# Attention in a two-block transformer kernel: one VectorE pass writes the masked, scaled scores to four SBUF places

## The reference

```
scores = q . k * 96 ** -0.5        # for one head: 1024 queries x 1024 keys
scores = where(key <= query, scores, -inf)
p      = exp(scores - max over keys) ; p = p / sum over keys
out    = p @ v
```

## Time and profile before

| | us |
|---|---|
| median of 3 runs | 2840.65 (2839.79 to 2842.64) |
| profiled execution, its own time | 2838.5 |
| span of its instructions | 2836.8 |
| PE busy | 2729.4 (96%) |
| DVE busy | 1814.4 (64%) |
| ACT busy | 1021.3 (36%) |
| POOL busy | 1277.9 (45%) |

### The profile page before, as it was taken

One profiled execution on the slowest core, in us unless ns is written; L12 is line 12 of the kernel. 1 busy time (PEld: TensorE's weight loads), 2 busy tenths in 40 slices (PEclk: granted clock), 3 DMA queues, 4 the chain that ended last, 5 costly groups with the idle time before them and its releaser, 6 DMA issues.

```text
span 2836.8 us, 32978 instructions
## 1 busy us (share of the span) xinstructions
PE 2729.4 (96%) x12578; PEld 2155.0 (76%) x12578; DVE 1814.4 (64%) x2070; ACT 1021.3 (36%) x1397; POOL 1277.9 (45%) x780
## 2 busy tenths in 40 slices
PE   7999999999999999999998999889998999999998
PEld 5888788787777888887786887555587788878777
DVE  3111355655747766669879758776637766777887
ACT  4000323332214333334444014665535433344444
POOL 2433322223436988884333444102332888833321
PEclk9999999999999999999999999999899999999999
DMA  5223232324442333336631534103333345565543
GB/s 180 96 95 108 88 119 90 119 90 156 148 141 79 100 112 102 90 118 215 205 115 49 187 112 117 33 33 97 102 127 104 119 141 163 173 206 163 163 134 134
DMA packets 336967, 348.90 MB, mean 123 GB/s; under 512 B 18915, under 2 KB 256602, under 8 KB 336822
## 3 DMA queue, kind: packets, MB, share of 16 engines
q1 hardware_dynamic: 327254, 311.30, 35.6%
q10 hardware_dynamic: 9568, 35.66, 3.2%
HBM read 237.53 MB, written 108.34 MB: 122 GB/s over the span
## 4 chain that ended last, share of the span: by engine, by line
PE 51%; DVE 10%; issue 2%; ACT 2%; DMA 1%; POOL 1%; SPq 0%; DVEq 0%; ACTq 0%; POOLq 0%
PE ps L3282 34%; PE ps L533 9%; DVE op_lo L3359 2%; PE ps L2367 1%; PE ps L2740 1%; DVE sw_lo L3192 1%; PE ps L2390 1%; DVE small L2321 1%; PE ps L2377 1%; DVE x L2312 1%; PE ps L2858 1%; DVE acc L3603 1%; DVE acc L3610 0%; PE ps L2713 0%; DVE acc L1889 0%
## 5 line engine op out<-in xcount | busy, mean ns | idle before, releaser
L3282 PE MATMUL ps<-op_hi,sw_hi 128*128 128x512 f32 x1769 | 692.6, 392 | 15.5 <-DVE op_lo L3359 8.2
L3282 PE MATMUL ps<-op_hi,sw_lo 128*128 128x512 f32 x1769 | 689.1, 390 | 0.0
L3282 PE MATMUL ps<-op_lo,sw_hi 128*128 128x512 f32 x1769 | 688.9, 389 | 0.0
L499 POOL TENSOR_TENSOR w_hi_t<-w_raw,ones 128x1024 fp32r<-128x1024 f32 (+1 forms) x85 | 162.1, 1910 | 735.7 <-PE ps L533 354.7
L3282 PEld LDWEIGHTS ps<-op_hi,sw_hi 128*128 128x128 f32 x1769 | 332.4, 188 | 96.8 <-issue 16.8
L3282 PEld LDWEIGHTS ps<-op_hi,sw_lo 128*128 128x128 f32 x1769 | 332.4, 188 | 69.2
L3282 PEld LDWEIGHTS ps<-op_lo,sw_hi 128*128 128x128 f32 x1769 | 332.6, 188 | 68.7 <-issue 0.5
L656 DVE TENSOR_TENSOR stage<-ps,rstd 128x1024 f32<-128x1024 f32 x62 | 75.8, 1222 | 345.4 <-PE ps L533 326.9
L3182 ACT ACTIVATE sw_hi<-sw_sumNone 128x512 fp32r<-128x512 f32 (+1 forms) x252 | 157.1, 624 | 330.3 <-PE ps L3282 247.0
L533 PE MATMUL ps<-h1hi,w_hi_t 128*128 128x512 f32 x720 | 233.5, 405 | 13.0 <-DVE h1lo L617 9.0
L3192 POOL TENSOR_TENSOR sw_lo<-sw_sumNone,sw_hi 128x512 fp32r<-128x512 f32 x138 | 214.7, 1565 | 33.2 <-ACT sw_hi L3182 33.1
(11 more groups left out here) (444 smaller groups left out, 4877.2 us busy)
## 6 DMA issues: line engine op xcount, KB each, us to landing
op_raw<-hidden SPq DMA_DIRECT2D x42, 1024.0 KB, 8.6
w_raw<-in_w_in SPq DMA_DIRECT2D x60, 512.0 KB, 3.9
sw_raw<-in_w_ffn_in SPq DMA_DIRECT2D x44, 512.0 KB, 5.3
proj<-stage ACTq DMA_DIRECT2D x42, 512.0 KB, 2.6
hidden<-hidden_blocks SPq DMA_DIRECT2D x13, 1536.0 KB, 6.2
acc<-proj SPq DMA_DIRECT2D x36, 512.0 KB, 4.5
hidden<-hidden_blocks SPq DMA_DIRECT2D x14, 1280.0 KB, 5.0
sw_raw<-in_w_up SPq DMA_DIRECT2D x32, 512.0 KB, 8.3
```

Source lines behind the costliest of these rows:

```text
L499: ins = pool.tensor_tensor(whi[:, u.par, s], raw[:, u.par, s], ones[:, 0:1].to_broadcast([P, n]), ALU.mult)
L3282: mm = pe.matmul(out, w, x[:, k, :], start=(k == 0 and i == 0 and r < 4), stop=(k == n - 1 and i == 2), skip_group_check=r >= 4)
```

## The change

DVE takes the scores with one instruction, `tensor_tensor_reduce`: out = (scores + mask_row) * (-scale), with the minimum over the row as a second output (starting from BIG). `out` is one of four places `x4[:, n % 4]` in SBUF. Since everything is negated, the minimum is minus the scaled maximum, and it serves as the bias as it stands. ACT takes the exponential of (bias minus that place), in place. The mask is now a row of 1024, zero but for the last 128 columns; its last N columns are added to the whole of the scores. POOL makes it in the earlier stage, behind L1944. `scores(n + 2)` waits for the pass of `n` (`s_stat`) and no longer for the exponential; the pass of `n` waits for `turn(n - 4)` (`pt_ready`). The small columns move (`sm`), `turned_p` gets places of its own, and two waits of the mLSTM on `p_ready` are on `s_stat`.

```diff
+        mask_row = at("mask_row", [P, T], R0 + 128)
...
                     pool.memset(cb[:, :, 0:3], 0.0).then_inc(S["ml_consts"], 1)
+                    pool.memset(mask_row[:, :], 0.0).then_inc(S["ml_consts"], 1)
+                    pool.wait_ge(S["ml_consts"], 2)
+                    last = mask_row[:, T - P:T]
+                    pool.affine_select(out=last, in_=last, compare_op=ALU.is_ge, fill=-BIG, base=0,
+                                       pattern=[[-1, P]], channel_multiplier=1).then_inc(S["ml_consts"], 1)
...
-        turned_p = [x4[:, 2, :], x4[:, 3, :]] + [at(f"p_turned{n}", [P, T], kb)[:, :] for n, kb in ((2, 107.5), (3, 111.5))]
+        turned_p = [at(f"p_turned{n}", [P, T], kb)[:, :] for n, kb in enumerate((75.03125, 107.5, 79.03125, 111.5))]
...
-                act.wait_ge(S["s_stat"], 2 * n + 2)
-                if n >= 2:
-                    act.wait_ge(S["pt_ready"], n - 1)
-                act.activation(x4[:, n % 2, 0:N], PS[n % 2][:, 0:N], ACT.Exp, bias=sm(n, 1), scale=QK_SCALE,
-                               accum_out=sm(n, 2)).then_inc(S["p_ready"], 1)
+                act.wait_ge(S["s_stat"], n + 1)
+                act.activation(x4[:, n % 4, 0:N], x4[:, n % 4, 0:N], ACT.Exp, bias=sm(n, 0), scale=-1.0,
+                               accum_out=sm(n, 1)).then_inc(S["p_ready"], 1)
...
+            dve.wait_ge(S["ml_consts"], 3)
+            dve.wait_ge(S["q_rope"], 8)
             for n, (h, i) in enumerate(NQ):
                 N = (i + 1) * P
                 dve.wait_ge(S["s_ready"], n + 1)
-                late = PS[n % 2][:, N - P:N]
-                dve.tensor_tensor(late, late, negm[:, :], ALU.add).then_inc(S["s_masked"], 1)
-                dve.wait_ge(*count("s_masked", n + 1))
-                dve.tensor_reduce(sm(n, 0), PS[n % 2][:, 0:N], AX.X, ALU.max).then_inc(S["s_stat"], 1)
-                dve.wait_ge(S["s_stat"], 2 * n + 1)
-                dve.tensor_scalar(sm(n, 1), sm(n, 0), -QK_SCALE, None, ALU.mult).then_inc(S["s_stat"], 1)
+                if n == 3:
+                    dve.wait_ge(S["vh_t"], 8)
+                if n >= 4:
+                    dve.wait_ge(S["pt_ready"], n - 3)
+                dve.tensor_tensor_reduce(x4[:, n % 4, 0:N], PS[n % 2][:, 0:N], mask_row[:, T - N:T], -QK_SCALE, BIG,
+                                         ALU.add, ALU.min, sm(n, 0)).then_inc(S["s_stat"], 1)
...
-                    pe.wait_ge(S["p_ready"], n - 1)
+                    pe.wait_ge(S["s_stat"], n - 1)
```

More of the change, by code:

```diff
@@ L246 @@
          "out_row": ("kdt_ready", 8), "x3_squared": ("g_step", 24), "x3_summed": ("conv_step", 16), "qk_high": ("yb_ready", 8),
-         "qk_low": ("yb_scaled", 8), "s_masked": ("o_sum", 8),
+         "qk_low": ("yb_scaled", 8),
          "x3_last_spilled": ("mv_loaded", 64)}
@@ L2227, in mla_act @@
                 if h == 7:
-                    act.activation(small[:, 44:45], ones[:, 0:1], ACT.Exp)
+                    act.activation(small[:, 52:53], ones[:, 0:1], ACT.Exp)
                 act.wait_ge(S["unit_done"], uk.times(1, 1))
@@ L2257, in sm @@
         def sm(n, what):
-            c = 40 + 5 * (n % 2) + what
+            c = 40 + 3 * (n % 4) + what
             return small[:, c:c + 1]
@@ L2309, in normalise @@
                 dve.wait_ge(S["p_ready"], n + 1)
-                dve.reciprocal(sm(n, 3), sm(n, 2)).then_inc(S["rs_inv"], 1)
+                dve.reciprocal(sm(n, 2), sm(n, 1)).then_inc(S["rs_inv"], 1)
                 dve.wait_ge(S["rs_inv"], n + 1)
-                dve.tensor_scalar(x4[:, n % 2, 0:N], x4[:, n % 2, 0:N], sm(n, 3), None, ALU.mult)\
+                dve.tensor_scalar(x4[:, n % 4, 0:N], x4[:, n % 4, 0:N], sm(n, 2), None, ALU.mult)\
                    .then_inc(S["p_norm"], 1)
+            dve.wait_ge(S["ml_consts"], 3)
+            dve.wait_ge(S["q_rope"], 8)
             for n, (h, i) in enumerate(NQ):
@@ L2376, in turn @@
                 for j in range(NQ[n][1] + 1):
-                    tr = pe.transpose(PS[2][:, j * P:(j + 1) * P], x4[:, n % 2, j * P:(j + 1) * P], ident[:, :])
+                    tr = pe.transpose(PS[2][:, j * P:(j + 1) * P], x4[:, n % 4, j * P:(j + 1) * P], ident[:, :])
                 tr.then_inc(S["pt_ready"], 1)
@@ L2679, in turn_v @@
             if h == 0:
-                pe.wait_ge(S["p_ready"], 64)
+                pe.wait_ge(S["s_stat"], 64)
             if h == 1:
@@ L2691, in weight_scores @@
             if n == 0:
-                pe.wait_ge(S["p_ready"], 63)
+                pe.wait_ge(S["s_stat"], 63)
             if J == 0:
```

## The result

| us | before | after |
|---|---|---|
| median of 6 runs each | 2840.86 (2839.79 to 2843.09) | 2826.53 (2819.55 to 2829.75) |
| profiled execution, its own time | 2838.5 | 2826.9 |
| span | 2836.8 | 2825.2 |

The ratio after to before is 0.9946, 95% interval 0.9933 to 0.9959. It is worked out from all runs; the two medians are 14.3 us apart (0.9950), where 9.5 was forecast. So the sign and the place were right, and the size was forecast too small.

A forecast was written before the change was run, and what follows sets the result against it. PE, busy for 96% of the span, was taken as the bound, so only its idle time could be won: 9.4 + 0.4 - 0.3 = 9.5 us less, 2829.0 us profiled, 2831.2 as median, forecast range 2827 to 2835.

The forecast's parts named there:

- the place: The one stage touched, 1780 to 1953.5 us, where PE lost 19.4 us to other engines inside the steps.
- the sum over PE's waits: In the steps, fourteen waits give 0.40 us each and twelve 3.79 together: 9.4 us less (7.6 to 10.1).
- the scores' gate: The scores' two waits for the exponential, 1.0 us, go as PSUM frees earlier; together 0.4 us won.
- the ring: In the steps PE and DVE wait for each other: transposes 15.5 us for DVE, DVE 35.1 for scores.
- The pass's rate: The new DVE pass costs what the running maximum costs: 1225 ns for 1024, 291 for 128.
- The first rival: The new DVE pass runs at half rate, as the scan does: slower, 2845.6 us, median 2847.8; chance 0.13.
- term s: What DVE's chain to the reciprocal loses per step: 0.44 - 0.05, about 0.40 us, ends 0.30 and 0.45.
- From N = 896 on PE's own work covers DVE's: In the steps' widest score rows, from N = 896 on, PE was said not to wait for DVE.
- the 26 waits: PE's transposes waiting for DVE's row multiplication, 15.5 us in all; fourteen above 0.45 us, twelve below 0.40.
- POOL's mask row: Filling the mask row on POOL in the earlier stage, 1.0 to 1.9 us; loss 0 to 1.2, taken 0.3.
- The whole shift should be passed on: The mLSTM behind the steps starts from their end, so the full 9.5 us should reach the total.
- the second rival: Gain made, but PE's clock takes part: one more low stretch of 10 us, 2836.2 us; chance 0.10.

The follow-up runs named there:

- e7: Changed kernel with two small DVE operations more (128 and 64 columns) between pass and reciprocal; 2846.09 us, ratio 1.0017 to the kernel before.
- e9: Changed kernel with one small DVE operation more (128 columns) between pass and reciprocal; 2830.22 us, ratio 0.9969 to the kernel before.
- e1: The changed kernel measured again without any edit; 2828.40 us, ratio 0.9957 to the kernel before, steps 159.6 us.
- e4: Kernel before without the mask's addition on DVE, so its output lacks the causal mask; 2831.68 us, ratio 0.9973 to the kernel before.
- e5: Changed kernel with the scores waiting for the exponential again, as before; 2825.56 us, ratio 0.9952 to the kernel before.
- e3: Changed kernel with three extra PE matmuls, results unused, at the start of the steps; 2828.02 us, ratio 0.9955 to the kernel before.
- e10: Changed kernel with four mLSTM pieces on DVE moved from steps 52, 53, 56 and 57 to 58 to 61; 2821.65 us, ratio 0.9933 to before.
- e12: The changed kernel measured once more without any edit; 2825.36 us, ratio 0.9947 to the kernel before, steps 157.1 us.
- e6: Changed kernel with two SBUF places in place of four, the pass waiting for the transposes of n - 2; 2845.01 us, ratio 1.0017 to before.
- e11: Kernel before with its exponential writing to four places in place of two, nothing else; 2839.80 us, ratio 1.0003 to the kernel before.
- e8: Kernel before with two extra PE matmuls, results unused, filling the idle gap at the steps' start in time; 2840.38 us, ratio 0.9998.

## Why the prediction was right in kind and wrong in size

The step that failed is the sum over PE's waits: 9.4 us, 9.8 with the scores' gate, where the steps got 13.9 us shorter at an equal clock. Both of its inputs were too small: what the chain loses, and what each wait is worth.

**The place and the ring.** Right. PE lost time in the steps only where its work ended before DVE's chain; a shorter chain shortened these waits (15.5 to 6.3 us) and turned up as DVE's wait for the scores (35.1 to 44.2). A longer chain brought them back (e7, e9).

**The pass's rate.** Right: 1225 ns for 1024, the maximum's. The Trainium skill, "DVE: opcode table, instruction layouts, handler registers and perf-mode slots", Datapath and trigger behaviour, says that a stage reading its own last result loses no cycle; the trace agrees, the slope is (1225 - 292) / 896 = 1.04 ns an element. The halving that the Trainium skill names in "Vector Engine (DVE) Microarchitecture Reference", Points that are easy to get wrong, is for two sources in SBUF; with one in PSUM the trace shows none. The first rival, half rate, is out.

**The term s was mis-sized.** The prediction put 0.05 us for the accumulator's write on the path, with 0.30 and 0.45 as ends, and took s = 0.40. Measured it is 0.52 at N = 768. The write takes 83 ns, and none of them lie on the path: the reciprocal starts in the same moment. And the start of both lies 0.08 us before the pass's end, while in the earlier trace rows the scaling stood 0.03 behind the maximum's end. The prediction counted the overlap of scaling and reciprocal as saved but not that of the pass and what follows it. 0.52 lies above the upper end of 0.45.

**The waits were read too short.** The idle time that PE's row prints is less than what the wait cost. PE's rows in order of time, before (the transposes behind the first row stand in the earlier trace rows, at 1892.10):

```profile
1890.16 1.67 PE L2367 MATMUL ps<-kT,acc 96*128 96x512 f32 x4
...
1896.73 1.88 PE L2367 MATMUL ps<-kT,acc 96*128 96x512 f32 x4
1898.76 0.98 PE L2377 MATMUL ps<-ident,x 128*128 128x128 f32 x7
```

and the same two places after:

```profile
1878.43 1.67 PE L2373 MATMUL ps<-kT,acc 96*128 96x512 f32 x4
1879.94 0.82 PE L2383 MATMUL ps<-ident,x 128*128 128x128 f32 x6
...
1884.52 1.88 PE L2373 MATMUL ps<-kT,acc 96*128 96x512 f32 x4
1886.24 0.93 PE L2383 MATMUL ps<-ident,x 128*128 128x128 f32 x7
```

Where nothing waits, the transposes' row starts 0.16 us before the scores' row ends, since matmuls are pipelined (1879.94 against 1878.43 + 1.67). So the wait printed as 0.27 at 1892.10 was 1.94 - 1.51 = 0.43 from start to start, and at N = 896 there was a wait of 2.03 - 1.72 = 0.31 for which no idle time is printed at all. That one the prediction denied in words: "From N = 896 on PE's own work covers DVE's."

Redone with both corrections, each of the 26 waits gives the smaller of its printed value plus 0.17 and 0.50 (s rounded down): twenty give 0.50, six give 2.59 together, and the four hidden ones, one in each pair, 0.31 each: 10.0 + 2.59 + 1.24 = 13.8 us. Measured: 13.9 in e1, with the clock as before. For e4 (0.34) the same rule gives 26 x 0.34 + 1.24 = 10.1, where 7.6 were measured, 10.1 by the estimate without the extra low clock. For e9 (0.32) it gives 9.6, where 8.4 were measured with one more low stretch (0.67 over 1904 to 1918) and a shorter first one, together some 3 us more than before: 9.5 by the same estimate. This rule was made after the result, from the same profiles. Of the error, s alone, put into the prediction's own sum, makes about 1.4 us (14 x 0.10); the larger part, about 3, comes from the reading of the waits.

The total fits better than its parts. By head pair the rule gives 2.25, 3.75, 3.58 and 4.25 us, and e1 gained 2.79, 3.25, 3.45 and 4.39 up to the last transposes of each. A wait is not a fixed stock, since PE's own start moves too. In step 52 the rule gives 0.50, yet the wait of 1.31 us is still 1.30 after: an instruction on DVE ahead of it (L2287 after) now waited for ACT, so that DVE and PE won only 0.32 us there, and PE's scores no longer waited 0.25 us for the exponential. The prediction counted that 0.25 beside the other wait, as a gain of its own; it lay inside it.

**The scores' gate**, 0.4 us forecast: up to 0.6 by e5, from one profile each. Of the first wait (0.71) some 0.14 us were won, near the 0.18 forecast; the 0.25 was counted twice, as said.

**POOL's mask row**, 0.3 us forecast, up to 1.2: nothing. The row in order of time on POOL, after:

```profile
1566.05 0.95 POOL L1946 MEMSET mask_row<- 128x1024 f32 x1
1567.15 0.43 POOL L1949 TENSOR_SCALAR_AFFINE_SELECT mask_row<-mask_row 128x128 f32<-128x128 f32 x1
1567.56 2.86 POOL L500 TENSOR_TENSOR w_hi_t<-w_raw,ones 128x1024 fp32r<-128x1024 f32 x1
...
1576.98 1.90 POOL L500 TENSOR_TENSOR w_hi_t<-w_raw,ones 128x1024 fp32r<-128x1024 f32 x1 [3.22 <-PE ps L534]
```

The two instructions cost 1.5 us on POOL, and the split right behind them took 2.86 us where it had taken 1.90; why is not shown. So 2.4 us of the spare time went, and not 1.0 to 1.9: POOL then had 3.22 us left where it had 5.64. The cover held. The kernel after was 0.56 us ahead of before already when this began, and 0.48 ahead at the first scores.

**"The whole shift should be passed on"** failed, in the other direction. The mLSTM took 2.6 to 2.7 us more in all three profiles of the kernel after, at a clock of 0.79 or 0.80. Its length goes with its granted clock through the profiles in the table, whatever the steps ahead of it were: 97.3 us at 0.89, 99.9 at 0.85, 101.4 to 101.8 at 0.83, 102.6 at 0.82, 104.2 to 104.3 at 0.80 and 0.79, some 0.8 us for 0.01. Only e3 lies off this row, with 102.7 at 0.80. The difference is in PE's busy time and not in its waits, as the mLSTM of e5 shows beside that of the kernel after:

```profile
1939.30:2036.60 97.30, 88.17 (x326) 51.27 (x323) 63.93 (x99) 52.94 (x68) 42.57 (x31) 0.89 0.46 133
```

PE was busy for 88.2 us and idle for 9.1; in the kernel after it was busy for 97.8 and idle for 6.4, with the same instructions. What sets the clock there was not found: e5 and e10 differ little from the kernel after in their steps, and have 0.89 and 0.85. Nor is it fixed for a kernel: one unprofiled execution each of the kernel after (2819.55) and of e12 (2820.09) had a mean clock of 0.990 over the whole program, as e5's profiled one, where the other executions of these three had 0.984 to 0.988. So something like the second rival, "given back", stands in these three profiles, in the mLSTM and at 2.6 us, about half of the 5 us that the rival put on it; that the change causes it is not shown. The rest behind the mLSTM varied between 781.9 and 785.5 us in kernels of both kinds, and these profiles don't tie it to the change.

**The early return of the clock** in two of three profiles (2.5 us) was not in the prediction.

The sum, in the prediction's terms: steps 13.9 to 16.4 for 9.8 forecast, POOL 0 for 0.3, given back 2.6 for 0, which makes 11.3 to 13.8; measured as medians 11.5, 13.9 and 14.3. That agreement is in part luck: the three profiled executions were 11.6, 9.4 and 13.1 us under the one of before, since the start and the rest behind the mLSTM, which the sum leaves out, moved as well.

## What to carry to other kernels

In a ring of two engines, what the slower side's chain loses is won once per wait, so count the waits and take the smaller of wait and saving; but measure a matmul's wait from start to start against the same pair of instructions where nothing waits, not by the printed idle time. This is an estimate for the total and not for the single wait (step 52). When several small dependent instructions are put into one, count also the overlap that the chain had hidden at its end. Fusing a pass moves where buffers are written: without more places (e6) the gain was lost whole, and the places alone (e11) gave nothing.

## What the runs showed of the hardware

- A custom pass on DVE with one f32 operand in PSUM, one in SBUF, a write to SBUF and a running minimum runs at 1.04 ns an element, as a plain maximum does, and the 83 ns of the write of its accumulator lie beside the next instruction.
- The low stretch of the granted clock at the start of the steps lasted about 10 us in one execution and about 3 in another of the same kernel (e1 against e12), and filling 1.73 of the idle 2.10 us ahead of it with matmuls did not shorten it (e8).
- The mLSTM, with the same instructions, took 97.3 to 104.3 us in the fourteen profiles, and PE's busy time in it rose from 88.2 to 97.8 us while its granted clock fell from 0.89 to 0.80 (e5 against the kernel after).
